# A last projection turned from channels as rows to tokens as rows, in two passes over the weight

## The chip, the cores and the metric

One core of one Trainium2 chip runs the whole program. The metric is device time in microseconds, from start to end of one execution. Five engines work beside each other and meet at semaphores: PE (TensorE), DVE (VectorE), ACT (ScalarE), POOL (GpSimd) and SP (SyncE, which here only issues DMAs).

## The reference

Two transformer blocks with float32 data, 1024 tokens of width 1024. The first holds attention, a short convolution, a state-space mixer and a feed-forward part, the second differential attention and an mLSTM. The change touches only the end of the second block:

```python
        merged = (jax.nn.sigmoid(ga) * jnp.einsum('bsw,wd->bsd', ya, w_a[l])
                 + jax.nn.sigmoid(gb) * jnp.einsum('bsw,wd->bsd', yb, w_b[l]))
        out = jnp.einsum('bsd,de->bse', merged, w_out[l])
        x = x + _rmsnorm(out, norm_post[l])
```

`_rmsnorm(out, g)` divides each token's row by the root of the mean of its squares over the 1024 channels (plus 1e-6) and multiplies by the gain `g`, which has one value for each channel.

## The kernel before, in words

Almost everywhere a tile is 128 channels (partitions) by 1024 tokens. Float32 products run in three TensorE matmuls: both operands are split into a rounded high part and a low rest (`HH`, `HL` for activations, `WH`, `WL` for weights), and high times high, high times low and low times high are added in PSUM. A "unit" is a 128x1024 piece of weight (512 KB). SP loads it into one of two slots of `WR` (line 498) as soon as that slot has been split. POOL splits it in two halves of 512 columns, each one addition (`WH`, line 522) and one subtraction (`WL`, line 525), into a ring of two slots. `w_used[0]` and `w_used[1]`, which PE raises when it has begun a later part, tell POOL that the first or the second half of a slot may be overwritten. `w_split` tells PE that a half is ready.

The end of the program before the change:

- **Merges.** For each of eight tiles of 128 channels PE makes two products of a half depth (`mixers`, 24 matmuls each, lines 607 to 613) and, two tiles ahead, two gate projections of full depth (48 matmuls each). Two PSUM slots of `PG` (1024 columns each) are used in turn, and `g.before` makes PE wait until the slot is free. ACT takes the sigmoids into `MS` and `MS2` (line 2007). DVE's `merge_tile` multiplies the first product (`MA`, line 2944) and the second (`MS2`, line 2947) and adds them into `RAW` (line 2951). Each of the first two frees a slot. The last two tiles have no gate projections behind them: their four products run back to back.
- **Split of merged.** When all eight tiles are in `RAW`, ACT copies each to `HH` (line 1437) and DVE subtracts for `HL` (line 2085).
- **Projection.** Output tiles have 128 output channels as rows and 1024 tokens as columns; the weight is stationary and 512 tokens move. `first_pair` (lines 638 to 646) makes two output tiles at once, block by block as `HL` arrives; the other six units come from `projection`, 48 matmuls each. Of each output tile ACT takes the squares (line 1424) and a copy with the gain (`OUT2`, line 1425), and DVE adds the squares up (line 2112).
- **x back.** ACT reloads x, stored in HBM with channels as rows, with one DMA of 4 MB, and PE transposes it through `PG` in eight token tiles of eight 128x128 transposes (line 723). ACT and DVE copy these to `XT`, which takes the place of `RAW`. This stands ahead of the last two units.
- **End.** PE sums the squares over the channels (line 1362), ACT takes roots, DVE reciprocals. PE transposes `OUT2` in eight token tiles, DVE scales each by its token's factor and adds x (line 2977), and ACT issues eight stores of y.

The order on each engine is the order of the code; nothing is scheduled by the program itself.

## Time and profile before

| | us |
|---|---|
| median of 3 runs | 2457.97 (2457.89 to 2461.23) |
| profiled execution, its own time | 2455.18 |
| its span in the profile | 2453.1 |
| PE busy | 2318.1 (94%) |
| DVE, ACT, POOL busy | 1157.5, 705.6, 987.8 |

The span is what the profiler saw; the time holds a little more around it. Busy PE is not PE at its peak, since ends of matmuls are modelled; the distance from one matmul's start to the next is what counts. The mean granted clock of TensorE was 0.984 of full speed (2.4 GHz).

### The profile page before, as it was taken

Reading aid. Unit: us, or ns where it says so; the run is one execution under the profiler, and the core shown is the slowest. Engines: PE = TensorE matmul, PEld = TensorE weight load, DVE = VectorE, ACT = ScalarE, POOL = GpSimd, SP = SyncE. Lnnn points to the kernel's source line nnn. Section 1 sums busy time; section 2 is a strip of 40 time slices with the busy share of each in tenths; the row PEclk is TensorE's granted clock in tenths of the full one; section 3 lists DMA queues with packets and bytes.
Section 4 is the critical chain, followed back from the end, with each engine's and each line's share of the span. In section 5 each row is a group of like instructions: output and inputs, shape, how many; then the busy total and the mean of one; then the engine's idle time right before and its main releaser. Section 6 shows DMA issues by size and latency. Waiting matters only on the chain.

```text
span 2453.1 us, 27542 instructions
## 1 busy us (share of the span) xinstructions
PE 2318.1 (94%) x9990; PEld 1762.4 (72%) x9990; DVE 1157.5 (47%) x1201; ACT 705.6 (29%) x1097; POOL 987.8 (40%) x789
## 2 busy tenths in 40 slices
PE   7999999899899999999999879999999998999998
PEld 5777755477788888888877656666676675888776
DVE  5774455545733433334337875465455444411223
ACT  4243355522311111111123423333423433200121
POOL 3533400186544444444436632222254451444340
PEclk9999999999999999999999999999999999999999
DMA  5111100222111111111112300000011110111121
GB/s 196 44 40 38 35 1 9 86 86 78 61 43 51 51 43 51 47 47 51 43 52 71 129 26 26 26 26 26 26 35 38 39 43 18 52 43 51 53 102 69
DMA packets 31186, 125.84 MB, mean 51 GB/s; under 512 B 3464, under 2 KB 3848, under 8 KB 30224
## 3 DMA queue, kind: packets, MB, share of 16 engines
q1 hardware_dynamic: 28656, 103.26, 13.0%
q10 hardware_dynamic: 2464, 21.66, 2.2%
q8 instruction: 46, 0.75, 0.1%
q14 instruction: 20, 0.16, 0.0%
HBM read 112.33 MB, written 12.58 MB: 51 GB/s over the span
## 4 chain that ended last, share of the span: by engine, by line
PE 81%; DVE 9%; ACT 4%; issue 4%; DMA 1%; POOL 1%; SPq 0%; DVEq 0%; ACTq 0%; POOLq 0%
PE PG L607 14%; PE PG L613 13%; PE PG L612 13%; PE PG L1134 5%; PE PG L1140 5%; PE PG L1139 4%; PE PG L954 2%; PE PG L1180 2%; PE PO L981 1%; PE PO L1203 1%; PE PT L968 1%; PE PO L1277 1%; PE PG L660 1%; PE PG L666 1%; PE PG L665 1%
## 5 line engine op out<-in xcount | busy, mean ns | idle before, releaser
L522 POOL TENSOR_TENSOR WH<-WR,zero 128x512 fp32r<-128x512 f32 x376 | 417.0, 1109 | 1335.1 <-PE PG L607 705.6
L525 POOL TENSOR_TENSOR WL<-WR,WH 128x512 fp32r<-128x512 f32 x376 | 535.2, 1423 | 29.4
L607 PE MATMUL PG<-HH,WH 128*128 128x512 f32 x1232 | 486.9, 395 | 3.7 <-issue 1.4
L613 PE MATMUL PG<-HH,WL 128*128 128x512 f32 x1232 | 480.4, 390 | 0.0
L612 PE MATMUL PG<-HL,WH 128*128 128x512 f32 x1232 | 480.1, 390 | 0.0
L607 PEld LDWEIGHTS PG<-HH,WH 128*128 128x128 f32 x1232 | 231.7, 188 | 58.5 <-issue 6.1
L612 PEld LDWEIGHTS PG<-HL,WH 128*128 128x128 f32 x1232 | 231.7, 188 | 49.7 <-issue 2.2
L613 PEld LDWEIGHTS PG<-HH,WL 128*128 128x128 f32 x1232 | 231.7, 188 | 48.7
L1134 PE MATMUL PG<-HH,WH 128*128 128x512 f32 x544 | 230.2, 423 | 5.4 <-ACTq L1881 2.8
L1140 PE MATMUL PG<-HH,WL 128*128 128x512 f32 x544 | 213.5, 392 | 0.0
L1139 PE MATMUL PG<-HL,WH 128*128 128x512 f32 x544 | 212.6, 391 | 0.0
L1134 PEld LDWEIGHTS PG<-HH,WH 128*128 128x128 f32 x544 | 102.9, 189 | 41.3 <-issue 13.8
L2166 DVE SCALAR_TENSOR_TENSOR VU<-PG,vec,VU 128x1023 f32<-128x1023 f32 (+1 forms) x42 | 53.8, 1282 | 161.4 <-ACT VU L1699 158.7
L2166 DVE SCALAR_TENSOR_TENSOR VG<-PG,vec,VG 128x1023 f32<-128x1023 f32 (+1 forms) x42 | 53.8, 1282 | 142.0 <-ACT VG L1699 138.8
L1139 PEld LDWEIGHTS PG<-HL,WH 128*128 128x128 f32 x544 | 103.0, 189 | 24.2 <-issue 4.8
L1140 PEld LDWEIGHTS PG<-HH,WL 128*128 128x128 f32 x544 | 102.4, 188 | 22.9
L1795 ACT ACTIVATE DP<-PG,cols 128x128 f32<-128x128 f32 (+7 forms) x64 | 47.3, 741 | 143.1 <-DVE cols L2726 90.1
L1711 ACT ACTIVATE GH<-PRD 128x1024 fp32r<-128x1024 f32 x20 | 21.2, 1062 | 228.4 <-PE PG L613 180.2
L1180 PE MATMUL PG<-DK,DQ 128*128 128x512 f32 (+3 forms) x192 | 72.7, 497 | 11.9 <-DVEq L2676 9.8
L2944 DVE TENSOR_TENSOR MA<-PG,MS 128x1024 f32<-128x1024 f32 x8 | 9.8, 1224 | 149.0 <-PE PG L613 149.0
L954 PE MATMUL PG<-KOP,QOP 128*128 128x512 f32 (+3 forms) x192 | 74.5, 509 | 3.4 <-ACTq L1629 2.4
L2477 DVE TENSOR_REDUCE cols<-PG 128x1 f32<-128x128 f32 (+7 forms) x64 | 48.3, 754 | 60.5 <-PE PG L958 60.3
(458 smaller groups left out, 3938.0 us busy)
## 6 DMA issues: line engine op xcount, KB each, us to landing
WR<-weights SPq DMA_DIRECT2D x188, 512.0 KB, 3.4
X<-x_spill ACTq DMA_DIRECT2D x2, 4096.0 KB, 12.4
RAW<-x SPq DMA_DIRECT2D x8, 512.0 KB, 7.8
x_spill<-X ACTq DMA_DIRECT2D x1, 4096.0 KB, 12.8
x_spill<-X ACTq DMA_DIRECT2D x4, 1024.0 KB, 5.0
y<-RAW ACTq DMA_DIRECT2D x8, 512.0 KB, 2.8
POSI<-positions ACTq DMA_DIRECT2D x1, 512.0 KB, 15.1
sqf<-squares SPq DMA_DIRECT2D x1, 256.0 KB, 2.6
```

The source lines that it names most:

```text
L522: pool.tensor_tensor(WH[:, slot, part], WR[:, slot, part], zero[:, :].to_broadcast([P, HALF]), ALU.add).then_inc(w_hi, 1)
L525: pool.tensor_tensor(WL[:, slot, part], WR[:, slot, part], WH[:, slot, part].bitcast(F32), ALU.subtract).then_inc(w_split, 1)
L607: m = pe.matmul(out[:, cut], WH[:, slot, w], hi[:, cut], start=n == 0, stop=False)
L612: pe.matmul(out[:, cut], WH[:, slot, w], lo[:, cut], start=False, stop=False)
L613: m = pe.matmul(out[:, cut], WL[:, slot, w], hi[:, cut], start=False, stop=last)
L954: m = pe.matmul(g.psum(n)[:, h * HALF:end], QOP[:, i % 2, hh, t * P:(t + 1) * P], KOP[:, 2 * i + hh, h * HALF:end], start=True, stop=end ! ...
L1134: m = pe.matmul(out, WH[:, slot, w], HH[:, b, cut], start=b == 0, stop=False)
L1139: pe.matmul(out, WH[:, slot, w], HL[:, b, cut], start=False, stop=False)
L1140: m = pe.matmul(out, WL[:, slot, w], HH[:, b, cut], start=False, stop=b == KT - 1)
L1180: pe.matmul(out[:, h * HALF:end], DQ[:, c, t * P:(t + 1) * P], DK[:, c, h * HALF:end], start=True, stop=end != (t + 1) * P)
L2166: ins = dve.scalar_tensor_tensor(out[:, d:], g.psum(k)[:, 0:S - d], w, out[:, d:], ALU.mult, ALU.add)
L2477: dve.reduce_max(cols[:, 2 + hh:3 + hh], g.psum(n)[:, 0:(t + 1) * P], AX.X, negate=True).then_inc(m_neg, 1)
```

## The change

The last projection computes rows of tokens. The 128x128 block of `HH` or `HL` (128 channels by 128 tokens) is stationary, and 512 output channels of one weight row block move. A unit is now a row block of the weight. Eight PSUM banks (`PT`, `PO` and both slots of `PG`) hold four token tiles of 128x1024 at a time, so the weight is read and split twice, in a first pass for tokens 0 to 511 and a second for 512 to 1023: 16 units, 24 matmuls each, where there were 8 of 48. Within a unit the order is by column halves, in the first and last ones by token tiles. In the second pass row block 7 is split early into a place of its own (`WXH`, `WXL`) and is used together with block 6, tile by tile, at the very end.

The norm's sum comes from the activation that squares a token tile (`accum_out`), one root and one reciprocal per tile. `OUT2` is the scaled and gained tile, to which DVE adds x. The gain is loaded by one DMA as a row for all partitions. x comes back in eight DMAs of 512 KB, paced by the units, and is transposed between the passes and within the second pass's first unit. y is stored by SP tile by tile, the last tile in two halves. DVE splits tiles 0 to 5 of merged ahead of the merge of tile 6, and tiles 6 and 7 each behind its merge.

```diff
-               ("merge", 3 * KT), ("out2", KT)]
+               ("merge", 3 * KT), ("out2", 2 * KT)]
...
                 ("ffn_last", 2 * KT), ("diff", 4),
-                ("merge_first", 2), ("merge", 4 * (KT - 2)), ("merge_last", 4), ("out2", KT - 2), ("x_back", TT), ("out2_last", 2), ("y", TT)]
+                ("merge_first", 2), ("merge", 4 * (KT - 2)), ("merge_last", 4)]
...
+OUT2_ORDER = [0, 1, 7, 2, 3, 4, 5, 6]
...
-        OUT2 = at("OUT2", 172, [P, KT, S])
+        OUT2 = at("OUT2", 172, [P, TT, D])
+        WXH = at("WXH", 152, [P, D], F32R)
+        WXL = at("WXL", 156, [P, D], F32R)
+        GAIN = at("GAIN", 160, [P, D])
         XT = RAW
...
+        def token_bank(t):
+            return (PTf, POf, PG[:, 0, :], PG[:, 1, :])[t % 4]
...
+            for t in range(TT - 1):
+                sp.wait_ge(o_done, t + 1)
+                sp.dma_start(y_out[t * P:(t + 1) * P, :], XT[:, t, :]).then_inc(y_stored, 16)
+            sp.wait_ge(o_done, TT)
+            sp.dma_start(y_out[(TT - 1) * P:, halves(0)], XT[:, TT - 1, halves(0)]).then_inc(y_stored, 16)
+            sp.wait_ge(y_stored, 16 * (TT + 1))
...
-            with pool.Fori(UNIT0["merge"] // 2 + 1, UNITS // 2) as i:
+            with pool.Fori(UNIT0["merge"] // 2 + 1, UNIT0["out2"] // 2 + 5) as i:
                 for n in range(2):
                     split(i, n)
+            def split_out2(n):
+                u, raw, place = UNIT0["out2"] + n, WR[:, n % 2, :], UNIT0["out2"] + n - 1
+                pool.wait_ge(w_loaded[n % 2], 16 * (u // 2) + 16)
+                for q in range(2):
+                    part = halves(q)
+                    if n == KT + 2:
+                        hi, lo = WXH[:, part], WXL[:, part]
+                    else:
+                        hi, lo = WH[:, place % 2, part], WL[:, place % 2, part]
+                        pool.wait_ge(w_used[q], place - 1 + q)
+                    pool.tensor_tensor(hi, raw[:, part], zero[:, :].to_broadcast([P, HALF]),
+                                       ALU.add).then_inc(w_hi, 1)
+                    pool.wait_ge(w_hi, 2 * u + q + 1)
+                    pool.tensor_tensor(lo, raw[:, part], hi.bitcast(F32), ALU.subtract).then_inc(w_split, 1)
+            pool.wait_ge(s_lo, SPLIT0["merged"] + KT)
+            for n in range(KT + 2, 2 * KT):
+                split_out2(n)
...
-            first_pair("out2", Groups("out2"), 0, "merged")
-            with pe.Fori(1, KT // 2 - 1) as i:
-                g = Groups("out2", i, 2)
-                for k in range(2):
-                    projection("out2", g, k, k, HH, HL, i, 2)
-            pe.wait_ge(x_back, 32)
-            turn_tiles(Groups("x_back"), X)
-            for k in range(2):
-                projection("out2", Groups("out2_last"), k, KT - 2 + k, HH, HL)
-            pe.wait_ge(n_sq, NORM_TILES0["post2"] + 1)
-            for t in range(TT):
-                m = pe.matmul(PO[:, 0, t:t + 1], SQ[:, 0, t * P:(t + 1) * P], ones[:, 0:1],
-                              start=True, stop=True)
-            m.then_inc(n_sq_used, 1)
-            Groups("out2_last").wait_free(pe, 0)
-            Groups("out2_last").wait_free(pe, 1)
-            turn_tiles(Groups("y"), OUT2)
+            def token_half(t, h, b, hi, lo, start=False, stop=False):
+                tokens, out, cut = slice(t * P, (t + 1) * P), token_bank(t)[:, halves(h)], halves(h)
+                first = pe.matmul(out, HH[:, b, tokens], hi[:, cut], start=start, stop=False)
+                pe.matmul(out, HH[:, b, tokens], lo[:, cut], start=False, stop=False)
+                last = pe.matmul(out, HL[:, b, tokens], hi[:, cut], start=False, stop=stop)
+                return first, last
+            def ring(place):
+                return WH[:, place % 2, :], WL[:, place % 2, :]
+            def by_columns(t0, b, u, place, before=lambda t: None):
+                for h in range(2):
+                    unit("out2", u, q=h)
+                    for t in range(t0, t0 + 4):
+                        if h == 0:
+                            before(t)
+                        first, _ = token_half(t, h, b, *ring(place), start=b == 0)
+                        if t == t0:
+                            first.then_inc(w_used[1 - h], 1)
+            def by_tokens(t0, b, u, place, before=lambda t: None):
+                unit("out2", u, q=1)
+                for t in range(t0, t0 + 4):
+                    before(t)
+                    for h in range(2):
+                        first, last = token_half(t, h, b, *ring(place), start=b == 0, stop=b == KT - 1)
+                        if t == t0 and h == 0:
+                            first.then_inc(w_used[1], 1)
+                        if t == t0 + 3 and h == 1:
+                            first.then_inc(w_used[0], 1)
+                    if b == KT - 1:
+                        last.then_inc(o_ready, 1)
+            def merged_out(t):
+                if t >= 2:
+                    Groups("merge_last").wait_free(pe, t)
+            for b in range(KT - 1):
+                pe.wait_ge(s_lo, SPLIT0["merged"] + b + 1)
+                by_columns(0, b, b, b, merged_out if b == 0 else lambda t: None)
+            wait_split("merged")
+            by_tokens(0, KT - 1, KT - 1, KT - 1)
+            def turn_x(t, bank, scaled=0, kept=0):
+                if scaled:
+                    pe.wait_ge(o_scaled, scaled)
+                if kept:
+                    pe.wait_ge(xt_kept, kept)
+                for k in range(KT):
+                    m = pe.transpose(token_bank(bank)[:, k * P:(k + 1) * P], X[:, k, t * P:(t + 1) * P], ident)
+                m.then_inc(xt_turned, 1)
+            pe.wait_ge(x_back, 16 + 16 * KT)
+            turn_x(0, 0, scaled=1)
+            turn_x(1, 1, scaled=2)
+            turn_x(2, 0, kept=1)
+            turn_x(3, 2, scaled=3)
+            turn_x(4, 1, kept=2)
+            turn_x(5, 3, scaled=4)
+            def beside(t):
+                if t > 4 and t < 7:
+                    turn_x(t + 1, t - 3, kept=2 * t - 6)
+                pe.wait_ge(xt_kept, (3, 5, 7, 8)[t - 4])
+            by_tokens(4, 0, KT, KT, beside)
+            for place in range(KT + 1, 2 * KT - 2):
+                u = place if place == KT + 1 else place + 1
+                by_columns(4, place - KT, u, place)
+            unit("out2", 2 * KT - 1, q=1)
+            for t in range(4, TT):
+                for h in range(2):
+                    token_half(t, h, KT - 2, *ring(2 * KT - 2))
+                    _, last = token_half(t, h, KT - 1, WXH, WXL, stop=True)
+                last.then_inc(o_ready, 1)
...
-            act.wait_ge(g_ready, GROUP0["out2"])
-            act.dma_start(X[:, :, :].rearrange("p k n -> p (k n)"), spill).then_inc(x_back, 16)
-            with act.Fori(0, KT // 2 - 1) as i:
-                for k in range(2):
-                    c = VEC0["norm_post_2"] + k
-                    out_tile(Groups("out2", i, 2), k, 2 * i + (SQUARE0["post2"] + k),
-                             OUT2[:, bass.ds(2 * i + k, 1), :], vec[:, bass.ds(2 * i + c, 1)])
-            g = Groups("x_back")
-            for t in range(0, TT, 2):
-                g.ready(act, t)
-                act.activation(XT[:, t, :], g.psum(t), ACT.Copy).then_inc(g.free(t), 1)
-            for k in range(2):
-                out_tile(Groups("out2_last"), k, SQUARE0["post2"] + KT - 2 + k, OUT2[:, KT - 2 + k, :],
-                         v("norm_post_2", KT - 2 + k))
-            act.wait_ge(n_sq_used, NORM_TILES0["post2"] + 1)
-            act.activation(cols[:, 0:TT], PO[:, 0, 0:TT], ACT.Sqrt, bias=v("eps"), scale=1.0 / D)\
-               .then_inc(n_root, 1)
-            g = Groups("y")
+            act.wait_ge(g_ready, GROUPS)
+            for k in range(KT):
+                act.wait_ge(w_used[1], UNIT0["out2"] + min(k, KT - 2) + 1)
+                act.dma_start(X[:, k, :], spill[:, k * S:(k + 1) * S]).then_inc(x_back, 16)
+            act.dma_start(GAIN[:, :], gain_in.to_broadcast([P, D])).then_inc(gain_in_place, 16)
+            def token_root(t):
+                act.wait_ge(o_ready, t + 1)
+                act.activation(T[:, t % 2, :], token_bank(t), ACT.Square, accum_out=cols[:, t:t + 1])\
+                   .then_inc(o_square, 1)
+                act.wait_ge(o_square, t + 1)
+                act.activation(cols[:, t:t + 1], cols[:, t:t + 1], ACT.Sqrt, bias=v("eps"), scale=1.0 / D)\
+                   .then_inc(o_root, 1)
+            for t in range(4):
+                token_root(t)
             for t in range(TT):
-                g.wait_free(act, t)
-                act.dma_start(y_out[t * P:(t + 1) * P, :], XT[:, t, :]).then_inc(y_stored, 16)
-            act.wait_ge(y_stored, 16 * TT)
+                act.wait_ge(xt_turned, t + 1)
+                act.activation(XT[:, t, :], token_bank((0, 1, 0, 2, 1, 3, 2, 3)[t]), ACT.Copy)\
+                   .then_inc(xt_kept, 1)
+            for t in range(4, TT):
+                token_root(t)
+            act.wait_ge(o_done, TT + 1)
+            act.dma_start(y_out[(TT - 1) * P:, halves(1)], XT[:, TT - 1, halves(1)]).then_inc(y_stored, 16)
+            act.wait_ge(y_stored, 16 * (TT + 1))
...
+            def split_merged(k0, k1):
+                t0 = SPLIT0["merged"]
+                primed(dve, g_done, k1)
+                for k in range(k0, k1):
+                    dve.sem_inc(s_raw, 1)
+                for k in range(k0, k1):
+                    dve.wait_ge(s_hi, t0 + k + 1)
+                    dve.tensor_tensor(HL[:, k, :], RAW[:, k, :], HH[:, k, :].bitcast(F32), ALU.subtract)\
+                       .then_inc(s_lo, 1)
+            dve.wait_ge(g_ready, GROUP0["merge_last"])
+            split_merged(0, KT - 2)
             for n in range(2):
                 merge_tile(Groups("merge_last"), 2 * n, n, KT - 2 + n)
-            primed(dve, g_done, KT)
-            split("merged", None, HL)
-            zero_sum()
-            sum_squares(KT // 2 - 1, SQUARE0["post2"])
-            g = Groups("x_back")
-            for t in range(1, TT, 2):
-                g.ready(dve, t)
-                dve.tensor_copy(XT[:, t, :], g.psum(t)).then_inc(g.free(t), 1)
-            for k in range(2):
-                add_square(SQUARE0["post2"] + KT - 2 + k, k)
-            end_sum("post2")
-            for t in (TT - 2, TT - 1):
-                g.wait_free(dve, t)
-            dve.wait_ge(n_root, NORM_INDEX["post2"] + 1)
-            step(dve.reciprocal(cols[:, 0:TT], cols[:, 0:TT]))
-            g = Groups("y")
-            for t in range(TT):
-                g.ready(dve, t)
-                dve.scalar_tensor_tensor(XT[:, t, :], g.psum(t), cols[:, t:t + 1], XT[:, t, :],
-                                         ALU.mult, ALU.add).then_inc(g.free(t), 1)
+                split_merged(KT - 2 + n, KT - 1 + n)
+            def scaled(t, columns=slice(0, D)):
+                return dve.scalar_tensor_tensor(OUT2[:, t, columns], token_bank(t)[:, columns], cols[:, t:t + 1],
+                                                GAIN[:, columns], ALU.mult, ALU.mult)
+            def added(t, columns=slice(0, D)):
+                dve.wait_ge(xt_kept, t + 1)
+                dve.tensor_tensor(XT[:, t, columns], OUT2[:, t, columns], XT[:, t, columns], ALU.add)\
+                   .then_inc(o_done, 1)
+            def factor(t):
+                dve.wait_ge(o_root, t + 1)
+                step(dve.reciprocal(cols[:, t:t + 1], cols[:, t:t + 1]))
+            dve.wait_ge(gain_in_place, 16)
+            for t in range(4):
+                factor(t)
+                scaled(t).then_inc(o_scaled, 1)
+            for t in range(TT - 1):
+                if t >= 4:
+                    factor(t)
+                    scaled(t).then_inc(o_scaled, 1)
+                dve.wait_ge(o_scaled, t + 1)
+                added(t)
+            factor(TT - 1)
+            for h in range(2):
+                step(scaled(TT - 1, halves(h)))
+                added(TT - 1, halves(h))
...
-    units.append(_blocks(a["w_out_2"][0], [tile(m * P) for m in range(KT)]))
+    rows = a["w_out_2"][0].reshape(KT, P, KT, P)
+    units += [rows, rows[OUT2_ORDER]]
```

## Rows read from the trace of the kernel before

**Rows 1.** The page: chain that ended last.
```profile
PE 81%; DVE 9%; ACT 4%; issue 4%; DMA 1%; POOL 1%; SPq 0%; DVEq 0%; ACTq 0%; POOLq 0%
```

**Rows 2.** Windows behind the merges: busy us by engine (instructions), granted clock, DMA.
```profile
2324.00:2353.20 29.20, 24.04 (x95) 19.48 (x95) 14.47 (x11) 8.10 (x9) 5.58 (x4) 0.88 0.40 162
2353.20:2399.40 46.20, 45.00 (x198) 36.61 (x197) 6.35 (x5) 9.65 (x11) 27.71 (x20) 1.00 0.14 46
2399.40:2409.70 10.30, 7.77 (x65) 6.76 (x64) 4.90 (x4) 6.01 (x6) 0.01 (x1) 1.00 0.01 2
2409.70:2431.50 21.80, 21.80 (x97) 17.77 (x96) 2.45 (x2) 2.03 (x2) 2.33 (x2) 1.00 0.00 1
2431.50:2453.10 21.60, 13.48 (x81) 11.82 (x80) 11.41 (x10) 3.58 (x4) 0.00 (x0) 0.79 0.48 194
```

**Rows 3.** Timeline of PE, with idle time before and its releaser.
```profile
1280.93 0.77 PE L1068 MATMUL PG<-GH,WH 128*128 128x512 f32 x1 [2.67 <-DVE VU L2166]
...
1352.60 1.13 PE L699 MATMUL PO<-SUM,sqf 128*128 128x512 f32 x2 [2.08 <-DVEq L2130]
...
2313.12 0.39 PE L607 MATMUL PG<-YH,WH 128*128 128x512 f32 x1
...
2323.77 0.39 PE L613 MATMUL PG<-YH,WL 128*128 128x512 f32 x1
2329.32 0.79 PE L638 MATMUL PG<-HH,WH 128*128 128x512 f32 x1 [5.16 <-DVE HL L2085]
...
2401.47 2.01 PE L723 MATMUL PG<-sqf,X 128*128 128x128 f32 x16 [1.25 <-ACT OUT L1425]
```

**Rows 4.** Windows of the two stretches behind waits of PE.
```profile
1285.00:1290.00 5.00, 5.00 (x19) 4.02 (x18) 0.82 (x2) 0.00 (x0) 0.15 (x1) 0.79 0.00 0
...
2327.70:2334.40 6.70, 5.08 (x12) 4.01 (x13) 6.36 (x4) 6.70 (x8) 3.25 (x2) 0.53 0.92 357
```

**Rows 5.** Timeline of DVE: two splits, a merge, the end.
```profile
2092.76 13.18 DVE L2085 TENSOR_TENSOR YL<-RAW,YH 128x1024 fp32r<-128x1024 f32 x8 [1.25 <-ACT YH L1437]
...
2307.94 1.22 DVE L2944 TENSOR_TENSOR MA<-PG,MS 128x1024 f32<-128x1024 f32 x1 [23.50 <-PE PG L613]
...
2328.04 11.11 DVE L2085 TENSOR_TENSOR HL<-RAW,HH 128x1024 fp32r<-128x1024 f32 x8 [1.18 <-ACT HH L1437]
...
2441.04 8.69 DVE L2977 SCALAR_TENSOR_TENSOR RAW<-PG,cols,RAW 128x1024 f32<-128x1024 f32 x7 [0.25 <-PE PG L723]
```

**Rows 6.** Timeline of ACT: root, sigmoid, split, last square.
```profile
20.03 0.20 ACT L1445 ACTIVATION_READ_ACCUMULATOR T<-RAW 128x1 f32 x1
20.25 1.28 ACT L1384 ACT_TABLE_LOAD   x1
...
21.54 0.30 ACT L1384 ACTIVATE cols<-cols,vec 128x8 f32<-128x8 f32 x1
...
2302.44 1.03 ACT L2007 ACTIVATE MS<-PG 128x1024 f32<-128x1024 f32 x1 [9.85 <-PE PG L613]
2326.96 1.06 ACT L1437 ACTIVATE HH<-RAW 128x1024 fp32r<-128x1024 f32 x1 [23.49 <-DVEq L2090]
...
2431.62 1.02 ACT L1424 ACTIVATE T<-PG 128x1024 f32<-128x1024 f32 x1 [8.85 <-PE PG L613]
```

**Rows 7.** Timeline of POOL: one half of a unit, beside merge 6.
```profile
2308.15 1.04 POOL L522 TENSOR_TENSOR WH<-WR,zero 128x512 fp32r<-128x512 f32 x1 [3.03 <-PE PG L607]
2309.27 1.29 POOL L525 TENSOR_TENSOR WL<-WR,WH 128x512 fp32r<-128x512 f32 x1
```

**Rows 8.** DMA issues, to landing: the page, then 2326 to 2345.
```profile
WR<-weights SPq DMA_DIRECT2D x188, 512.0 KB, 3.4
...
POSI<-positions ACTq DMA_DIRECT2D x1, 512.0 KB, 15.1
...
X<-x_spill ACTq DMA_DIRECT2D x1, 4096.0 KB, 12.5
WR<-weights SPq DMA_DIRECT2D x1, 512.0 KB, 7.4
```

More of the change, by code:

```diff
@@ L70 @@
 HALF0, _ = starts(STAGE_HALVES)
-NORMS = [("mix_pre", 1), ("q", 2), ("kv", 1), ("ssd", 2), ("post2", 1)]
-POST_SQUARES = [("mix_post", 2 * KT), ("ffn_post", 2 * KT), ("post2", KT)]
+NORMS = [("mix_pre", 1), ("q", 2), ("kv", 1), ("ssd", 2)]
+POST_SQUARES = [("mix_post", 2 * KT), ("ffn_post", 2 * KT)]
 SQUARE0, _ = starts(POST_SQUARES)
@@ L86 @@
 VECTORS = [("norm_mix_pre", 8), ("norm_mix_post", 8), ("norm_ffn_pre", 8), ("norm_ffn_post", 8),
-           ("norm_pre_2", 8), ("norm_post_2", 8), ("mla_q_norm", 2), ("mla_kv_norm", 1),
+           ("norm_pre_2", 8), ("mla_q_norm", 2), ("mla_kv_norm", 1),
            ("ssd_norm", 2), ("sc_conv", 2 * 3), ("ssd_conv", 6 * 5), ("dt_bias", 1), ("a_log", 1),
@@ L94, with program @@
 CONVOLVED = [0, 2, 4, 1, 3, 5]
+OUT2_ORDER = [0, 1, 7, 2, 3, 4, 5, 6]
 SQUARES = ["ident", "ones", "below", "rope_sum", "ahead"]
-def program(nc, wts, x_in, pos, vec_in, sq_in, aug_in, lam_in, y_out):
+def program(nc, wts, x_in, pos, vec_in, sq_in, aug_in, lam_in, gain_in, y_out):
     spill = nc.dram_tensor("x_spill", (P, KT * S), F32).ap()
@@ L286, in program @@
         g_sig, g_done = sem("g_sig"), sem("g_done")
-        x_back = sem("x_back")
+        x_back, gain_in_place = sem("x_back"), sem("gain_in_place")
+        o_ready, o_square, o_root, o_scaled, o_done = (sem(n) for n in (
+            "o_ready", "o_square", "o_root", "o_scaled", "o_done"))
+        xt_turned, xt_kept = sem("xt_turned"), sem("xt_kept")
         y_stored = sem("y_stored")
@@ L1418, in out_half @@
                    .then_inc(g.free(m), 1)
-            def out_tile(g, k, n, dst, scale=1.0):
-                g.ready(act, k)
-                primed(act, sq_sum, n - k % 2)
-                act.activation(T[:, k % 2, :], g.psum(k), ACT.Square).then_inc(sq_new, 1)
-                act.activation(dst, g.psum(k), ACT.Copy, scale=scale).then_inc(g.free(k), 1)
             def split(name, hi):
@@ L2103, in _ @@
                   "y": YH, "merged": HH}
-            def zero_sum():
-                step(dve.memset(SQ[:, 0, :], 0.0))
-            def add_square(n, k):
-                dve.wait_ge(sq_new, n + 1)
-                primed(dve, sq_sum, n)
-                dve.tensor_tensor(SQ[:, 0, :], SQ[:, 0, :], T[:, k, :], ALU.add).then_inc(sq_sum, 1)
-            def end_sum(post):
-                primed(dve, sq_sum, SQUARE0[post] + dict(POST_SQUARES)[post])
-                dve.sem_inc(n_sq, 1)
             def zero_halves():
@@ L2156, in chain_low @@
                                   ALU.subtract).then_inc(c_lo, 1)
-            def sum_squares(pairs, n0):
-                with dve.Fori(0, pairs) as i:
-                    for k in range(2):
-                        add_square(2 * i + (n0 + k), k)
             def taps(g, k, out, weights, then):
@@ L2966, in _ @@
-            for k in range(2):
-                add_square(SQUARE0["post2"] + KT - 2 + k, k)
-            end_sum("post2")
-            for t in (TT - 2, TT - 1):
-                g.wait_free(dve, t)
-            dve.wait_ge(n_root, NORM_INDEX["post2"] + 1)
-            step(dve.reciprocal(cols[:, 0:TT], cols[:, 0:TT]))
-            g = Groups("y")
-            for t in range(TT):
-                g.ready(dve, t)
-                dve.scalar_tensor_tensor(XT[:, t, :], g.psum(t), cols[:, t:t + 1], XT[:, t, :],
-                                         ALU.mult, ALU.add).then_inc(g.free(t), 1)
+                split_merged(KT - 2 + n, KT - 1 + n)
@@ L2981 @@
 _VECTORS_P = ("norm_mix_pre", "norm_mix_post", "norm_ffn_pre", "norm_ffn_post", "norm_pre_2",
-              "norm_post_2", "mla_q_norm", "mla_kv_norm", "ssd_norm")
+              "mla_q_norm", "mla_kv_norm", "ssd_norm")
 def _blocks(w, columns):
@@ L3137 @@
         "lambda_qk": a["lambda_qk_2"].reshape(1, 4 * 64),
+        "gain_row": a["norm_post_2"].reshape(1, D),
     }
```

## The prediction

> **What bounds the kernel now.** I read the page first, then the end of the trace by windows, then that end engine by engine as timelines, and last the DMA issues. The page says that the chain that ended last is 81% PE [rows 1], so time is won only where PE waits, crawls, or where something runs behind its last matmul. The change leaves everything up to the last merge products alone, so I budget from there. Tile 7's 48 products start at 2313.12 and the last of them at 2323.77 [rows 3]: 10.65 us for 47 steps is 0.2266 us from matmul to matmul, and the merges end at 2324.0. From there to the end of the span it is 129.1 us, in the five windows of [rows 2]. The reader is to see how they differ: 29.2 us for the first two units, 46.2 for four, 10.3 for the transposes of x, 21.8 for two units, 21.6 for an end with hardly a large matmul. The projection has 8 x 48 = 384 matmuls, 384 x 0.2266 = 87.0 us. The other 42.1 us are:
>
> - 5.3 us in which PE waits for `HL` tile 0 (2324.0 to 2329.32, the idle time and releaser stand in [rows 3]);
> - about 2.6 us of slow clock behind that wait: the granted clock is 0.53 until 2334.4, which is mostly the 1.2 GHz level [rows 4]; the 5.1 us in which PE was busy did what takes half of that at 2.4 GHz;
> - about 2.3 us between the first pair and the next units (29.2 + 46.2, less 5.3, 2.6 and 6 x 10.88 for six units, leaves 2.2 to 2.3);
> - 10.3 us for x back, 21.6 us for the end.
>
> **The matmuls.** The change has 16 units of 24 instead of 8 of 48: again 384, again a 128x128 stationary block and 512 moving columns, again a PSUM bank changed every three matmuls, as in the first pair. I take 87.0 us for them. A unit now lasts 24 x 0.2266 = 5.44 us.
>
> **The splits ahead of merge 6 (removes 5.3, adds a wait).** Tiles 0 to 5 are split when the last gate projection is done, at 2302.4. ACT first makes its sigmoid, to 2303.5, and its first copy takes 1.06 [rows 6], so DVE's first subtraction starts at about 2304.7. Eight subtractions took 11.1 us once and 13.2 us once, the second time with more POOL work beside them [rows 5]; six take 8.3 to 9.9 us, and end at 2313.0 to 2314.6. Beside them POOL splits a half of a unit at 2308.15, 1.04 and 1.29 us [rows 7]. Behind them in DVE's queue stands `MA` of tile 6, 1.22 us, which ran at 2307.94 before [rows 5]. It frees the PSUM slot that tile 7's first product wants at 2313.12 [rows 3]. It will end at about 2314.3 to 2315.9, and PE resumes 0.1 us later. So PE stalls 1.3 to 2.9 us, in a place where it did not wait before; I take 2.3, since POOL has a second subtraction in progress when the splits start. Merge 7 then ends with its own product and its `HL` is wanted only by the unit at the end of the first pass, 38 us later. Bounds: 0.1 us if nothing on POOL slows DVE (six at 1.2, then `MA`), 4.7 us if every POOL operation there costs DVE a whole operation of 2.3.
>
> Here the trace shows POOL and DVE slow each other, and the Trainium skill has the rule (SBUF — State Buffer, on the shared port pair): a DVE operation with two SBUF inputs and a GpSimd operation that reads SBUF hold the pair in turn, whole instruction by whole instruction. The 13.2 us against 11.1 agree with it. By the rule alone, two POOL operations would cost 2.3 us on top of six at 1.2, a stall of about 2.6 us instead of 2.3.
>
> **The first pass: 8 units, no wait for weights.** POOL needs 1.04 + 1.29 and about 0.1 between, 2.45 us for each half [rows 7], against 2.72 us of PE for a half unit: covered, but at 90%, where it was 45%. A half may be written 8.2 us before PE needs it. SP loads a slot again after its split, 3.4 us to landing [rows 8]; two units of PE are 10.88 us, a split and a load 4.9 + 3.4 + some waits. Cost 0; if the load took the 7.4 us seen beside the 4 MB of x [rows 8], 12.3 us for 10.88, 0.7 us a unit, about 5 us in the pass. x comes in pieces of 512 KB once a unit and is there before its transposes. The gain row queues behind the last two pieces; `POSI`, a broadcast row of the same size, landed 15.1 us after its issue, but behind a 4 MB store of some 12.5 us, so 3 us of its own [rows 8]. It is issued 10 us ahead of its use: 0.
>
> **Between the passes: 11.2 us (was 10.3).** Times from the first pass's start. Tile 0 is whole at 39.4, the pass ends at 43.5. ACT squares tile 0 (39.7 to 40.8), loads a table (1.28), takes the root (0.3) [rows 6]: 42.4. DVE's reciprocal and scaling (0.2, 0.15 and 1.28; seven scalings took 8.69 in [rows 5]) end at 44.2. PE's transposes of x tile 0 into that bank start 0.8 us late. Sixteen transposes take 2.01 us [rows 3], so a tile about 1.05. Tile 1 follows at 45.9 (its scaling ends 45.8), tile 2 at 48.4, since ACT first does the other three squares and roots (1.6 each, to 47.2) and then a copy of 1.03; tiles 3 to 5 without waits to 52.4. In the next unit two more tiles of transposes and about 0.5 of waits: the unit ends at 60.15, where nine units alone are 48.96. Difference 11.2; bounds 8.4 (eight tiles without a wait) and 14 (every tile waits for a copy of 1.03 and a hand-over, half of it hidden).
>
> Of the table load the row shows 1.28 us from the read of the sum to the root, with nothing between [rows 6]. In the Trainium skill (ScalarE: Activation LUTs, What ACT_TABLE_LOAD costs) a switch is about 2.66 us, with a drain. By that PE's first transposes would start 1.4 us later. The row decides.
>
> **The second pass.** 43.5 us with its first unit. POOL splits row block 7 at once behind unit 9 and stays ahead; the adds of x in DVE (two SBUF inputs) may slow a few halves by 1 us each, within the 5 us that POOL is ahead: 0, bound 2.
>
> **The end: 9.5 us (was 21.6).** The four tiles finish 2.72 us apart. DVE needs 0.2 + 0.15 + 1.28 + 0.15 + 1.23 = 3.0 a tile, so it runs up a little: tile 6 is done 2.9 us after the last matmul starts its drain, while tile 7's root is there at 1.8. Then reciprocal 0.35 and four operations of half a tile (0.7, 0.65 and 0.15 between): to 6.3. From DVE's last operation to the end of the span it was 2453.1 - 2449.7 = 3.4 us [rows 5]; I take 3.2 for half the bytes. Gone are the column sums, the eight transposes and seven of the eight scalings behind them. Bounds 8.5 and 11.5.
>
> **Slow clock: 2.6 us.** PE's waits of 2.67 and 5.16 us had slow stretches behind them (0.79 and 0.53 granted [rows 3, 4]), a wait of 2.08 us had none that the windows show. The new stall of 2.3 lies between, and the waits between the passes add up to 2.7 within 5 us. I charge one such stretch as before, 2.6 us; bounds 0 and two, 6.8 us.
>
> **Sum.** 2324.0 + 2.3 + 87.0 + 11.2 + 9.5 + 2.6 = 2436.6 against 2453.1: 16.5 us less. The profiled execution took 2455.18 with 2.1 around its span, so its counterpart is 2438.7. The median is 2.8 above it; 2457.97 - 16.5 = 2441.5.
>
> **The rivals.**
>
> - *Nothing stalls.* DVE's splits end before 2313 and PE never falls to 1.2 GHz, and x back costs its old 10.3: 2.2 + 2.6 + 0.9 more, 2435.8. For it: the clock held through x back before (1.00 in [rows 2]). Against it: DVE's queue order. Chance 0.14.
> - *The moved wait takes most back.* The stall is 4.7 and both places get a long slow stretch: 2.4 + 4.2 less gain, 2448.1. For it: every overlap of the two engines in the splits. Against it: only one half of a unit falls into them. Chance 0.13.
> - *Weights bound both passes (the other side).* The weight is read twice and a unit has half the time. If a slot's cycle, split 5.2 with hand-overs plus landing, exceeds 10.88, each unit costs half the excess. From a landing of 5.7 us it costs; at 8.0 us the gain is gone (14 units x 1.15 = 16.1), and above that the kernel is slower: at 9 us by 7 us, 2465. For it: 7.4 us beside a large transfer [rows 8]. Against it: x in small pieces, and 3.4 as the rule. Chance 0.04.
> - *It does less than it says at the end.* Roots and scalings queue behind each other so that the end stays near 14 us and the middle near 14: 2448.8. Chance 0.05.
>
> My forecast has 0.64, with a range of its own from 2438 to 2446. The range for 8 in 10 takes in half of the first two rivals on each side and the bounds: 2435 to 2450. A difference of 0.2% (4.9 us) is what a measurement of this kernel can tell from none. Faster 0.94, same 0.03, slower 0.03.
>
> **What would show it.** In the new trace: `MA` of tile 6 at about 2313.5 instead of 2307.94, and PE idle 2 to 3 us ahead of tile 7's products; the first unit right behind the last merge product; matmuls 0.227 apart through the first pass and POOL's halves 2.72 apart; some 11 us more than matmul time around the transposes; last matmul to end about 9.5 us. It would be wrong if PE waits for POOL's `WL` in a pass, if the matmuls with tokens stationary came slower than 0.2266 (at 0.24 it is 5 us), or if the clock stays at 1.2 GHz through the transposes.

## The result and the profile after

The changed kernel takes 2433.58 us (median of 4, 2429.38 to 2435.18) against 2457.93: ratio 0.9904, interval 0.9892 to 0.9916. It is faster, by 24.4 us where 16.5 were forecast, and 1.4 us below the stated range. A second set of five gave 2431.41 and 0.9909 (0.9895 to 0.9922).

Medians of one kernel differ by 2 to 3 us here, so I read stages from the traces, all counted from the start of ACT's last gate sigmoid (2302.44 before [rows 6], 2304.98 after). From there to the end of the span it was 150.7 us and is 127.1 us, 23.6 less. The second profile of the same changed kernel gives 127.1 again, though its sigmoid starts at 2299.6. What lies in front of that point wanders; what lies behind it was the same within 0.02 us in these two profiles. (One profile below, with the same code in that place, was 1.6 us off there.) Of the 24.4 us in the medians 23.6 are thus seen in the stages; 0.8 are within the wandering.

The windows of the changed kernel, busy us of PE, PEld, DVE, ACT and POOL with instructions, then granted clock and DMA. They answer to [rows 2].

```profile
2317.60:2328.50 10.90, 10.85 (x48) 9.01 (x49) 5.03 (x4) 1.06 (x1) 5.53 (x4) 1.00 0.16 50
2328.50:2372.00 43.50, 43.50 (x194) 35.98 (x192) 6.55 (x5) 4.75 (x7) 36.41 (x30) 1.00 0.61 199
2372.00:2388.20 16.20, 14.73 (x97) 12.51 (x96) 10.05 (x11) 10.56 (x16) 10.29 (x9) 1.00 0.16 51
2388.20:2425.00 36.80, 36.80 (x163) 30.20 (x161) 6.42 (x8) 4.23 (x9) 22.71 (x20) 1.00 0.37 132
2425.00:2432.10 7.10, 0.06 (x1) 0.00 (x0) 4.50 (x7) 1.41 (x3) 0.00 (x0) 0.83 0.52 205
```

The first pass is 43.5 us for 43.5 us of matmuls, at full clock, and the second is as dense behind its first unit. The end went from 21.6 to 7.1. From the last gate sigmoid on, PE has four waits longer than 0.2 us. They are these, from its timeline (answering to [rows 3]):

```profile
2317.65 0.47 PE L645 MATMUL PG<-YH,WH 128*128 128x512 f32 x1 [1.83 <-DVE MA L3024]
...
2372.75 1.06 PE L1442 MATMUL PT<-sqf,X 128*128 128x128 f32 x8 [0.42 <-DVE OUT L3056]
2374.05 1.09 PE L1442 MATMUL PO<-sqf,X 128*128 128x128 f32 x8 [0.23 <-DVE OUT L3056]
2375.96 1.09 PE L1442 MATMUL PT<-sqf,X 128*128 128x128 f32 x8 [0.82 <-ACT RAW L2135]
2376.89 1.04 PE L1442 MATMUL PG<-sqf,X 128*128 128x128 f32 x8
```

The 5.16 us before the first unit have become 1.83 before tile 7, as DVE's timeline explains: `MA` of tile 6 stands behind six subtractions (compare [rows 5]). Four of the six took 1.21 to 1.39 us each. The other two, which ran while POOL split a half unit (2310.70 to 2314.15), took 2.06 and 2.31.

```profile
2307.36 9.01 DVE L3045 TENSOR_TENSOR HL<-RAW,HH 128x1024 fp32r<-128x1024 f32 x6 [20.38 <-ACT HH L1531]
2316.29 1.21 DVE L3024 TENSOR_TENSOR MA<-PG,MS 128x1024 f32<-128x1024 f32 x1
```

The last token tile on ACT and DVE. Its root is there at 2426.53, and DVE is busy with the tile before up to that point.

```profile
2425.10 1.02 ACT L2125 ACTIVATE T<-PG 128x1024 f32<-128x1024 f32 x1 [1.28 <-PE PG L1393]
2426.02 0.19 ACT L2125 ACTIVATION_READ_ACCUMULATOR T<-PG 128x1 f32 x1
2426.24 0.29 ACT L2128 ACTIVATE cols<-cols,vec 128x1 f32<-128x1 f32 x1
```
```profile
2423.85 0.17 DVE L3068 RECIPROCAL cols<-cols 128x1 f32<-128x1 f32 x1
2424.05 1.28 DVE L3056 SCALAR_TENSOR_TENSOR OUT<-PG,cols,GAIN 128x1024 f32<-128x1024 f32 x1
2425.37 1.23 DVE L3062 TENSOR_TENSOR RAW<-OUT,RAW 128x1024 f32<-128x1024 f32 x1
2426.57 0.17 DVE L3068 RECIPROCAL cols<-cols 128x1 f32<-128x1 f32 x1
2426.77 0.75 DVE L3056 SCALAR_TENSOR_TENSOR OUT<-PG,cols,GAIN 128x512 f32<-128x512 f32 x1
...
2428.94 0.69 DVE L3062 TENSOR_TENSOR RAW<-OUT,RAW 128x512 f32<-128x512 f32 x1
```

### The profile page after: what moved, and what is told of

The parts are those of the page before. It is cut to its first block, busy times and chain, and to the rows that moved or that the text cites. A ratio compares the mean times of both kernels' runs of the same rounds, so it can differ in the third digit from the quotient of the medians.

```text
span 2432.1 us, 27427 instructions
## 1 busy us (share of the span) xinstructions
PE 2306.5 (95%) x9910; PEld 1752.2 (72%) x9910; DVE 1157.1 (48%) x1205; ACT 703.9 (29%) x1108; POOL 1023.7 (42%) x821
## 4 chain that ended last, share of the span: by engine, by line
PE 82%; DVE 9%; ACT 5%; issue 3%; DMA 1%; POOL 1%; SPq 0%; DVEq 0%; ACTq 0%; POOLq 0%
PE PG L645 13%; PE PG L651 13%; PE PG L650 13%; PE PG L1172 5%; PE PG L1178 5%; PE PG L1177 5%; PE PG L992 2%; PE PG L1218 2%; PE PO L1019 1%; PE PO L1241 1%; PE PT L1006 1%; PE PO L1315 1%; PE PG L698 1%; PE PG L704 1%; PE PG L703 1%
## 5 line engine op out<-in xcount | busy, mean ns | idle before, releaser
L645 PE MATMUL PG<-HH,WH 128*128 128x512 f32 x1136 | 449.2, 395 | 2.5 <-issue 1.4
L651 PE MATMUL PG<-HH,WL 128*128 128x512 f32 x1136 | 442.9, 390 | 0.0
L650 PE MATMUL PG<-HL,WH 128*128 128x512 f32 x1136 | 442.8, 390 | 0.0
L645 PEld LDWEIGHTS PG<-HH,WH 128*128 128x128 f32 x1136 | 213.7, 188 | 53.0 <-issue 6.1
L650 PEld LDWEIGHTS PG<-HL,WH 128*128 128x128 f32 x1136 | 213.6, 188 | 46.0 <-issue 2.2
L651 PEld LDWEIGHTS PG<-HH,WL 128*128 128x128 f32 x1136 | 213.7, 188 | 44.9
L1172 PE MATMUL PG<-HH,WH 128*128 128x512 f32 x544 | 231.2, 425 | 5.4 <-ACTq L1975 2.8
L1178 PE MATMUL PG<-HH,WL 128*128 128x512 f32 x544 | 214.2, 394 | 0.0
L1177 PE MATMUL PG<-HL,WH 128*128 128x512 f32 x544 | 213.4, 392 | 0.0
L1172 PEld LDWEIGHTS PG<-HH,WH 128*128 128x128 f32 x544 | 103.6, 190 | 42.2 <-issue 14.5
L1177 PEld LDWEIGHTS PG<-HL,WH 128*128 128x128 f32 x544 | 103.7, 191 | 24.4 <-issue 4.8
L1178 PEld LDWEIGHTS PG<-HH,WL 128*128 128x128 f32 x544 | 102.8, 189 | 22.9
L2952 DVE SCALAR_TENSOR_TENSOR MP<-PG,MD 128x1024 f32<-128x1024 f32 (+7 forms) x32 | 24.2, 757 | 96.1 <-PE PG L1306 57.1
```

What stands on the lines that cost most here:

```text
L645: m = pe.matmul(out[:, cut], WH[:, slot, w], hi[:, cut], start=n == 0, stop=False)
L650: pe.matmul(out[:, cut], WH[:, slot, w], lo[:, cut], start=False, stop=False)
L651: m = pe.matmul(out[:, cut], WL[:, slot, w], hi[:, cut], start=False, stop=last)
L1172: m = pe.matmul(out, WH[:, slot, w], HH[:, b, cut], start=b == 0, stop=False)
L1177: pe.matmul(out, WH[:, slot, w], HL[:, b, cut], start=False, stop=False)
L1178: m = pe.matmul(out, WL[:, slot, w], HH[:, b, cut], start=False, stop=b == KT - 1)
```

## The experiments

Three theories run through the expectations. Theory A: each part is worth what its stage shows, and slow clock follows long waits of PE. Theory B: slow clock does not depend on the wait. Theory C: the early splits carry most of the gain.

The table gives the stages of one trace of each kernel, in us: **a** last gate sigmoid to the last merge product, **b** from there to the first matmul of the projection, **c** to the first transpose of x, **d** to the last large matmul, **e** to the end of the span. Ratios are to the kernel before, with intervals; they are too wide to tell most of these kernels apart, so the readings go by the stages.

| kernel | a | b | c | d | e | sum | ratio |
|---|---|---|---|---|---|---|---|
| before | 21.33 | 5.55 | 69.86 | 32.01 | 21.96 | 150.71 | 1 |
| changed | 23.44 | 0.23 | 44.10 | 51.92 | 7.45 | 127.14 | 0.9904 (0.9892 to 0.9916) |
| changed again | 23.44 | 0.23 | 44.10 | 51.90 | 7.45 | 127.12 | 0.9909 (0.9895 to 0.9922) |
| splits alone | 23.42 | 0.22 | 67.56 | 32.00 | 20.39 | 143.59 | 0.9974 (0.9965 to 0.9984) |
| splits late | 21.33 | 5.55 | 46.75 | 51.91 | 7.44 | 132.98 | 0.9924 (0.9909 to 0.9939) |
| merges between splits | 21.34 | 0.22 | 44.10 | 51.90 | 7.44 | 125.00 | 0.9902 (0.9889 to 0.9915) |
| one more subtraction | 26.30 | 0.22 | 44.10 | 51.90 | 7.45 | 129.98 | 0.9925 (0.9906 to 0.9945) |
| three more | 30.02 | 0.22 | 44.10 | 51.92 | 7.44 | 133.70 | 0.9929 (0.9912 to 0.9946) |
| tiles together | 23.45 | 0.22 | 44.10 | 51.91 | 11.32 | 131.00 | 0.9914 (0.9897 to 0.9931) |
| last tile whole | 23.41 | 0.23 | 44.10 | 51.90 | 7.69 | 127.33 | 0.9910 (0.9896 to 0.9924) |
| gain first | 23.44 | 0.23 | 43.52 | 52.50 | 6.80 | 126.49 | 0.9911 (0.9893 to 0.9930) |
| both | 21.34 | 0.22 | 43.53 | 52.49 | 6.82 | 124.40 | 0.9905 (0.9885 to 0.9924) |
| one transpose | 25.06 | 0.23 | 44.10 | 50.68 | 7.44 | 127.51 | 0.9907 (0.9890 to 0.9923) |
| copies between | 21.33 | 0.23 | 43.52 | 51.07 | 6.81 | 122.96 | 0.9892 (0.9875 to 0.9908) |

**The changed kernel again.** 

> The changed kernel itself, for a second set of times beside the kernels that follow. Both theories: 0.990 of the kernel before, 2433 to 2435 us, PE's stall ahead of merge tile 7 near 1.8 us, no slow clock behind it.

127.12 us against 127.14, a wait of 1.82 us as in the first profile (1.83) and no slow clock behind it.

**The order of splits alone**, in the kernel before:

```diff
-            for n in range(2):
-                merge_tile(Groups("merge_last"), 2 * n, n, KT - 2 + n)
-            primed(dve, g_done, KT)
-            split("merged", None, HL)
...
+            dve.wait_ge(g_ready, GROUP0["merge_last"])
+            split_merged(0, KT - 2)
+            for n in range(2):
+                merge_tile(Groups("merge_last"), 2 * n, n, KT - 2 + n)
+                split_merged(KT - 2 + n, KT - 1 + n)
```

(`split_merged` is as in the change.) 

> The kernel before with the new order of splits alone (tiles 0 to 5 ahead of merge 6), the old projection kept. Theory A (each part is worth what its stage shows, and the slow clock follows the length of PE's wait): the wait of 5.2 us and 2.6 us of slow clock go, a stall of about 2 comes: 5.9 us less, 0.9976. Theory B (the slow clock is a matter of phase, independent of the wait): 3.3 us less, 0.9987. Theory C (the early splits carry most of the gain of the change): 12 us less or more, 0.995.

7.1 us less by the stages: 3.2 from wait against stall (a and b), 2.3 of slow clock in c, and 1.6 in e. That last part is slow clock too: the granted clock at the end was 0.86 on the mean against 0.79 in [rows 2], and the column sums took 1.95 us instead of 3.57, first in the kernel before, then here:

```profile
2434.01 3.57 PE L1362 MATMUL PO<-sqf,SQ 128*128 128x1 f32 x16 [2.43 <-DVEq L2116]
```
```profile
2430.99 1.95 PE L1362 MATMUL PO<-sqf,SQ 128*128 128x1 f32 x16 [2.43 <-DVEq L2116]
```

The code of the end is the same in both, so I don't count these 1.6 us as the splits' doing. Theory C is out: the splits carry 5.5 of the 23.6 us. In c there are still 2.3 us beyond six units (67.56 - 65.3). Most of them, 1.7, lie at two waits right behind the first pair, 0.84 us for ACT's `OUT` and 0.34 us for POOL's `WL`, with PE's slower start behind each; 0.4 are in the first pair. No such wait is in the changed kernel, where c is 43.5 and a wait of 0.42.

**All splits behind the last merge**, in the changed kernel (the edit above reversed). 

> The changed kernel with all eight splits behind the last merge, as before. Theory A: PE waits 5.2 us ahead of the first unit instead of 1.8 ahead of tile 7, and 2.6 us of slow clock come back: 6 us more than the changed kernel, ratio 0.993. Theory B: 3.4 us more, 0.992. Theory C: 12 us more, 0.995.

5.8 us more, as theory A has it. PE and then the windows around its wait (the granted clock is the third column from the end):

```profile
2330.70 0.79 PE L1391 MATMUL PT<-WH,HH 128*128 128x512 f32 x1 [5.16 <-DVE HL L2183]
```
```profile
2328.00:2332.00 4.00, 1.30 (x3) 1.11 (x4) 2.82 (x4) 3.67 (x4) 0.42 (x1) 0.66 0.00 0
2332.00:2336.00 4.00, 4.00 (x11) 3.02 (x11) 4.00 (x3) 4.00 (x5) 2.83 (x2) 0.50 0.43 131
```

**Merge products between the splits.**

```diff
-            split_merged(0, KT - 2)
-            for n in range(2):
-                merge_tile(Groups("merge_last"), 2 * n, n, KT - 2 + n)
-                split_merged(KT - 2 + n, KT - 1 + n)
...
+            lows(0, 2)
+            merge_tile(Groups("merge_last"), 0, 0, KT - 2, lambda: lows(2, 4))
+            lows(4, KT - 2)
+            split_merged(KT - 2, KT - 1)
+            merge_tile(Groups("merge_last"), 2, 1, KT - 1)
+            split_merged(KT - 1, KT)
```

(`lows` is the loop of subtractions; the function given to `merge_tile` runs between its two products.) 

> The changed kernel, DVE's queue reordered: splits of tiles 0 and 1, first product of merge 6, splits 2 and 3, second product and sum, splits 4 and 5, and so on. Theory A (the 1.83 us stall is the first product's place in DVE's queue): stall gone, 1.8 to 2.0 us less than the changed kernel, 0.9896. Rival: the split of tile 6 or 7 or POOL's weight halves come late instead and PE waits as long at the first unit: no difference.

The stall is gone, 2.1 us less, and nothing came in its place. DVE takes `MA` of tile 6 as soon as it is there:

```profile
2307.07 2.52 DVE L3057 TENSOR_TENSOR HL<-RAW,HH 128x1024 fp32r<-128x1024 f32 x2 [20.38 <-ACT HH L1531]
2310.20 1.23 DVE L3024 TENSOR_TENSOR MA<-PG,MS 128x1024 f32<-128x1024 f32 x1 [0.60 <-issue]
2311.46 3.45 DVE L3057 TENSOR_TENSOR HL<-RAW,HH 128x1024 fp32r<-128x1024 f32 x2
```

**A longer stall.** The subtraction of tile 5 is done once more (or three times more) with the same result:

```diff
+                    for _ in range(1 if k == KT - 3 else 0):
+                        step(dve.tensor_tensor(HL[:, k, :], RAW[:, k, :], HH[:, k, :].bitcast(F32),
+                                               ALU.subtract))
```

> The changed kernel with one split subtraction done twice ahead of merge 6, so that the stall before tile 7 grows from 1.8 by 1.3 to 3.1 us. Theory A (slow clock follows the length of the wait, and 2.67 us had one): 1.3 us more plus 1.7 to 3.4 of slow clock, 3 to 4.7 more than the changed kernel. Theory B (phase): 1.3 more in most runs.

> The same with the subtraction done four times: stall 1.8 + 3.9 to 5.0 = 5.7 to 6.8 us. Theory A: 4 to 5 more plus 2.6 to 3.4 of slow clock, 7 to 8 us above the changed kernel. Theory B: 4 to 5 above.

The waits became 3.08 and 5.60 us. Stage a grew by 2.86 and 6.58, so slow clock cost 1.6 and 2.8 us on top of waits 1.25 and 3.8 us longer. Both sums lie a little below what theory A foretold (3 to 4.7 and 7 to 8 us more) and well above theory B (1.3 and 4 to 5). A window of each kernel behind its wait, one more first:

```profile
2320.00:2324.00 4.00, 4.00 (x12) 3.17 (x11) 2.67 (x3) 1.06 (x1) 2.65 (x2) 0.60 0.10 13
```
```profile
2324.00:2328.00 4.00, 4.00 (x12) 3.14 (x11) 1.79 (x2) 1.06 (x1) 1.71 (x1) 0.56 0.29 55
```

**Second pass in plain order.** `OUT2_ORDER` is 0 to 7, all blocks go through the ring, and the pass ends with `by_tokens(4, KT - 1, 2 * KT - 1, 2 * KT - 1)` like the first. 

> The changed kernel with the second pass in the plain order of row blocks: block 7 is not kept aside, and the four tiles finish 1.36 us apart instead of 2.72. DVE needs 2.72 us for a tile. Theory A: three tiles queue on DVE, 3 x 1.36 = 4.1 us more from the last matmul to the end (7.2 to 11.3), all of it in the time, 2438. Rival (DVE is not what the end waits for, it is ACT's square and root at 1.5 a tile): under 1 us more.

3.9 us more, all in e (the median, 2434.86, shows less of it than the 2438 foretold). ACT is through with the last root at 2427.15, but DVE works its queue off:

```profile
2426.86 0.29 ACT L2102 ACTIVATE cols<-cols,vec 128x1 f32<-128x1 f32 x1
```
```profile
2425.77 0.16 DVE L3042 RECIPROCAL cols<-cols 128x1 f32<-128x1 f32 x1
...
2428.43 0.16 DVE L3042 RECIPROCAL cols<-cols 128x1 f32<-128x1 f32 x1
...
2431.08 0.15 DVE L3042 RECIPROCAL cols<-cols 128x1 f32<-128x1 f32 x1
```

Here, where tiles queue up, DVE's own pace is 2.66 us a tile, and 3 x (2.66 - 1.36) is the 3.9 us. So the early split of row block 7 is worth 3.9 us: it spaces the tiles 2.72 us apart, just above what DVE needs for one.

**Last tile whole.** One scaling, one addition and one store of 512 KB instead of halves. 

> The changed kernel with the last token tile scaled, added and stored whole instead of in two halves. Theory A: DVE's two whole operations 2.5 us instead of four halves 3.1, one store of 512 KB landing in about 2.9 instead of 2.5 us: within 0.5 us of the changed kernel, rather faster. Rival (halving hides the first half's store): 0.7 us more.

0.24 us more in e, between the two. From the reciprocal on, the halves cost DVE 3.06 us instead of 2.74, which is 0.3 more, and the end of the span is 2.5 us behind DVE's last operation instead of 3.0, which is 0.5 less.

**Gain first.** DVE multiplies by the gain as soon as ACT has squared, and applies the factor together with the addition:

```diff
-                return dve.scalar_tensor_tensor(OUT2[:, t, columns], token_bank(t)[:, columns], cols[:, t:t + 1],
-                                                GAIN[:, columns], ALU.mult, ALU.mult)
...
+                dve.wait_ge(o_square, t + 1)
+                dve.tensor_tensor(OUT2[:, t, :], token_bank(t), GAIN[:, :], ALU.mult).then_inc(o_scaled, 1)
...
-                dve.tensor_tensor(XT[:, t, columns], OUT2[:, t, columns], XT[:, t, columns], ALU.add)\
-                   .then_inc(o_done, 1)
+                dve.scalar_tensor_tensor(XT[:, t, columns], OUT2[:, t, columns], cols[:, t:t + 1],
+                                         XT[:, t, columns], ALU.mult, ALU.add).then_inc(o_done, 1)
```

> The changed kernel with the gain multiplied straight behind ACT's square (the factor is not needed for it) and the factor applied in one operation with the addition of x. Theory A: between the passes a bank is free a root and a reciprocal earlier, which takes 0.4 + 0.2 of PE's waits away; at the end DVE's work behind the last root falls from 3.1 to 1.7 us, while its multiplication (1.23) partly overlaps the root: 0.8 less. Together 1.0 to 1.5 us less than the changed kernel. Rival: the queue of DVE is full at the end (2.72 us a tile) and nothing is gained there: 0.5 less.

0.65 us less, not 1.0 to 1.5. All of it is at the end, where the rival had nothing. Between the passes nothing is won: PE starts 0.58 earlier and meets the loss at one place, the copy that frees the first bank.

```profile
2370.69 1.09 PE L1442 MATMUL PT<-sqf,X 128*128 128x128 f32 x8 [1.54 <-ACT RAW L2135]
```

Theory A was wrong about the middle: the waits shown there were steps of one chain through ACT. From ACT's first square to this point it is 7.7 us here (2363.01 to 2370.69) and in the changed kernel (2368.29 to 2375.96).

**Both reorderings.** 

> The gain first and DVE's queue reordered as in the experiment with merge products between the splits. Theory A: the savings add, 3 us less than the changed kernel, 2430.6, ratio 0.989. Rival: one eats the other's, under 2 us.

2.74 us less in the stages; the savings add (2.14 and 0.65). The times do not show it: the median is 2430.27, against 2431.41 of the changed kernel's second set.

**One transpose per tile.** Seven of eight transposes of x are left out, so most of x is missing from y. 

> The changed kernel with one 128x128 transpose of x per token tile instead of eight (the other seven eighths of x are left out; the copies and additions stay). It asks what the 9.25 us between the passes are made of. Theory A: PE's transposes, 8 tiles x 7/8 of 1.0 = 7.6 us at most, but PE would then wait for ACT's copies, eight at 0.91 us behind the four roots, so only about 3 to 4 us go. Rival (the transposes alone set it): 7 us go.

Only 1.24 us went in d. The second pass starts 5.12 us behind the first transpose instead of 6.68, which is 1.56: ahead of the pass, ACT's four squares and roots and its copies take almost as long as PE's transposes. Two more tiles of transposes lie within the pass. What they save does not show, since PE, idle in between, fell to the slow clock (0.50), and the first matmuls of the pass came 0.43 us apart instead of 0.23, about 1.8 us in all. Without the slow clock some 3 us would have gone (1.24 + 1.8, an estimate from these spacings), in line with theory A. This run also shows something unasked: the wait of 1.82 us ahead of tile 7, harmless in six profiles, had a slow stretch behind it here, 1.6 us in a.

```profile
2316.27 0.47 PE L645 MATMUL PG<-YH,WH 128*128 128x512 f32 x1 [1.82 <-DVE MA L3024]
```
```profile
2316.00:2320.00 4.00, 3.73 (x11) 3.01 (x12) 2.76 (x3) 0.97 (x1) 3.10 (x2) 0.66 0.02 4
...
2376.00:2380.00 4.00, 3.25 (x9) 2.10 (x10) 4.00 (x4) 4.00 (x6) 1.03 (x1) 0.50 0.00 0
```
```profile
2378.12 0.77 PE L1391 MATMUL PT<-WH,HH 128*128 128x512 f32 x1 [0.31 <-ACT RAW L2135]
2378.69 0.63 PE L1392 MATMUL PT<-WL,HH 128*128 128x512 f32 x1
2379.11 0.63 PE L1393 MATMUL PT<-WH,HL 128*128 128x512 f32 x1
```

**Copies between the squares**, on top of both reorderings:

```diff
-            for t in range(4):
-                token_root(t)
...
+            squared(0)
+            rooted(0)
+            for t in (1, 2):
+                squared(t)
+            x_tile(0)
+            squared(3)
+            x_tile(1)
+            for t in (1, 2, 3):
+                rooted(t)
...
```

(`squared` and `rooted` are the halves of `token_root`, `x_tile` is the copy of a turned tile of x; the other copies and roots follow in the old order.) 

> Both reorderings of before (merge products between the splits, gain first) and ACT's order changed: x tiles 0 and 1 are copied between the squares, the roots of tiles 1 to 3 come behind. Theory A: PE's one wait of 1.54 us between the passes goes, since the bank of tile 0 comes back while ACT would have taken roots: 1.2 to 1.5 us less than with both reorderings, 125.2 - 1.3 from the last gate sigmoid to the end where the changed kernel takes 127.1, that is about 123.1. Rival: the wait moves to tiles 6 and 7, nothing gained.

The wait is gone: 122.96 us, 1.44 less than with both reorderings (124.40) where 1.2 to 1.5 were foretold, and 4.2 us better than the changed kernel by the stages. (The 125.2 in the expectation is a slip: 123.1 follows from 124.4 - 1.3.) It has the lowest median of all, 2429.19, but its interval overlaps that of the changed kernel.

```profile
2371.85 1.09 PE L1442 MATMUL PO<-sqf,X 128*128 128x128 f32 x8
2372.86 1.09 PE L1442 MATMUL PT<-sqf,X 128*128 128x128 f32 x8
2373.78 1.04 PE L1442 MATMUL PG<-sqf,X 128*128 128x128 f32 x8
```

## Why the prediction was right and wrong

The direction, the places and the mechanisms held; the sum was 7.0 us short, since every term but the matmuls was charged too high. The steps that failed are four terms that were mis-sized, all the same way, above all the slow clock (2.6 us charged, 0 measured) and the end (9.5 charged, 7.2 measured).

- *384 matmuls, 87.0 us*: right. The first pass is 43.5 us, and POOL and the loads never held PE up; the rival of the weights did not come.
- *Stall ahead of tile 7, 2.3*: 2.1 (21.33 to 23.44 in a, with 1.83 idle). The row of splits gave 8.3 to 9.9 for six, it was 9.0, and the two slow ones were those beside POOL. That DVE's queue order is the cause is shown by its removal with the merges between the splits.
- *Slow clock, 2.6*: 0, the largest miss. The sum charged a stretch that I had called uncertain; the bounds had it at 0. Over the runs a wait of 1.8 us had one in one profile of seven (the changed kernel twice, splits alone, tiles together, last tile whole and gain first without, one transpose with), waits of 3.08, 5.16 and 5.60 in each of theirs. That the changed kernel's two profiles had none is thus in part luck. The part of the program that no experiment touched says more; see the last section. So length decides for long waits, and at 1.8 us it does not: neither theory A nor B alone.
- *Between the passes, 11.2*: 9.25 (b to d of the changed kernel, 96.25, less 87.0). ACT's square and root are 1.32 apart, not 1.6, three times; the transposes of a tile start 0.87 to 0.93 after those before, not 1.05. The row of 16 in 2.01 us [rows 3] runs to the modelled end of its last transpose, and I read it as a rate. The place of the waits was as foretold. The table load took 1.28 as in the row, with the root right behind it, not the 2.66 of the Trainium skill (ScalarE: Activation LUTs, What ACT_TABLE_LOAD costs).
- *The end, 9.5*: 7.2 (e less 0.23 for the last matmul). Counted from 0.23 us behind the last matmul's start (2424.90), the root was there at 1.6, about when I said (1.8), but DVE was free at 1.7, not at 2.9. A tile costs it 2.66 to 2.72, since each instruction starts 0.04 us behind the end of the one before, or ahead of it, where I had added 0.15 for each wait and got 3.0. That is 1.2 us; the reciprocal and the four half operations took 3.06 for 3.4, and the end of the span is 2.5 us behind DVE's last operation instead of 3.2.

The table load, from ACT's timeline of the changed kernel:

```profile
2369.21 0.19 ACT L2125 ACTIVATION_READ_ACCUMULATOR T<-PT 128x1 f32 x1
2369.42 1.28 ACT L2128 ACT_TABLE_LOAD   x1
2370.72 0.30 ACT L2128 ACTIVATE cols<-cols,vec 128x1 f32<-128x1 f32 x1
```

The range failed because its lower end summed the kinder bounds of two terms and a little of the middle's, and because the end's own bound, 8.5, was above the 7.2 that it took. The 2.3 us between first pair and next units were on my list of what there is and rightly in no term of the new kernel.

Of the 23.6 us, 14.5 are the end, 3.2 wait against stall, 2.3 to 2.6 the slow clock behind the old wait, 2.3 the old first pair and what follows it, and about 1 the transposes. Experiments stand behind the wait, the stall, its slow clock and 3.9 us of the end (the order of row blocks). The rest is read from the stages: no run takes the column sums or the transposes of the output alone out of the old end, and 1.6 of the 14.5 us are slow clock that splits alone did not have there.

## What to carry to other kernels

When work is moved ahead of another's queue, look at what frees a buffer behind it: here a reordering of one queue gave the stall back for nothing. Give the last tiles of a product the spacing that the finishing engine needs, and do what does not depend on the reduction while it runs. When summing many small terms by rows, do not take a group's length as its rate, and do not add a hand-over for each wait: three roundings to the safe side and one uncertain term charged in full made 7 us.
